# Hybrid decoder step: low parts subtracted before the next normalisation, the rest terms taken earlier, and the next layer's weight split behind the last normalisation

## Chip, cores and metric

The kernel runs on one core of a Trainium2 chip. The metric is the device time of one execution in microseconds (us).

## What is computed

The reference is one inference step of a 2-layer decoder for 512 prompt tokens and 64 sample tokens (8 sequences of 8), with D = 1024 channels. Cut to what matters here, each layer does

```python
mod = silu(c) @ w_ada[i] + b_ada[i]            # sh1, sc1, g1, sh2, sc2, g2
h = x * (1 + sc1) + sh1
mix = mixer(h @ w_in)                          # attention and convolution, then @ w_out
x = layernorm(ALPHA * x + g1 * mix)
h = x * (1 + sc2) + sh2
f = (silu(h @ w_gate) * (h @ w_up)) @ w_down
x = layernorm(ALPHA * x + g2 * f)
```

So there are four layer normalisations. The first three are each followed by a modulation of x to h and a projection of h, the last one by the output.

## The kernel before

**Layout.** Activations lie feature-major: `x` is 128 partitions x 8 tiles x 576 tokens. The two halves of 288 tokens are the columns of each matmul. All products are done in three parts to keep fp32 accuracy: weights and activations are split into a high part (a rounded copy, made by ScalarE) and a low part (the difference, made by VectorE), and TensorE adds high x high, low x high and high x low. A "unit" is one 128-column strip of weights over 8 tiles, 48 matmuls of 288 columns.

**Queues.** Each engine has its own order, written out by hand, and waits on semaphores. SyncE issues every transfer (`fetch` for weight units into the two buffers of `w_raw`, `around` for all else, among it the load of the layer's vectors `vec` after unit 1, which waits for `vec_used`). ScalarE makes `w_hi` (`split`, L500 to L507), which waits for the weights and for a free `w_hi` buffer of three. VectorE makes `w_lo` (`split`, L825 to L832), which frees the `w_raw` buffer for the next transfer.

**Normalisation.** The mean over the first six tiles is taken off early (`norm_first`). What is left of the mean, the rest, is subtracted by `take_rest` on VectorE, from sums in PSUM. `norm_last` on ScalarE loads the square root's table (L556), copies the row sums of squares (L558), squares the last tile (L547), squares the rest (L561) and takes the root (L563). VectorE takes the rest off tiles 0 to 2, reduces, takes the reciprocal (L966) and takes the rest off tiles 3 and 4. TensorE spreads the reciprocals over the partitions (L1310), and `normalise` multiplies each tile (L980). For tiles 5 to 7 it first takes the rest off that tile and waits for it.

**Modulation.** ScalarE scales the prompt tokens of a tile into one of three `hf` buffers (L519) and GpSimd the sample tokens (L463, L464); ScalarE rounds the tile to `h_hi` (L526); VectorE writes `h_lo` (L854), which frees the `hf` buffer. TensorE's `products_by_tile` (L1250) takes the tiles as their low parts come, for two units: 6 matmuls for each of tiles 0 to 3, 12 for each of tiles 4 to 7, and 24 for the second unit's last four tiles. `modulate` on VectorE puts the normalisations (`scale`) in between the low parts, two tiles ahead, and one weight split (`ahead`). For the first modulation of the kernel there is no normalisation and no split in it.

**Layer border.** After the last w_down product of layer 0, ScalarE makes the high part of layer 1's third unit (`split(l, UL + 2)`) and then `norm_last(l, 1)`. For the last layer that split returns at once.

Of the kernel before, what the change touches and what calls it, by code (L numbers as in the profile page):

```python
# [30 lines left out]
KT = D // P  # L31
# [77 lines left out]
NCEN = len(CENTRED)  # L109
# [41 lines left out]
def need(eng, sem, n):  # L151

    if n > 0:
        eng.wait_ge(sem, n)


def trunk(nc, xT, cT, ba_d, w_ada, w_mix, w_dn, kc_d, vc_d, st_d, vec_d, rope_d, eye_d, mp_d, msc_d, msn_d,
          y_d, k_d, v_d, cp_d, cs_d):
    with ExitStack() as ctx:
# [3 lines left out]
        s = {}  # L163
# [12 lines left out]
        def nth(l, name, k):  # L176

            return l * PER[name] + k + 1
# [106 lines left out]
        def halves(t):  # L285
            return t.rearrange("p (h n) -> p h n", h=2)
# [8 lines left out]
        def z_taken(l, z0, k):  # L295

            return l * ZL + z0 + k + 1
# [147 lines left out]
        def x_ready(eng, l, q, kt):  # L445

            if l == q == 0:
                eng.wait_ge(s["mod_ready"], 1)
                eng.wait_ge(x_in[kt // (KT // 2)], 16)
            else:  # L450
                eng.wait_ge(s["x_hat"], (2 * l + q - 1) * KT + kt + 1)
# [46 lines left out]
        def _(act):  # L498

            def split(l, u):  # L500

                g = l * UL + u
                if g >= DEPTH * UL:
                    return
                act.wait_ge(w_in[g % NR], 16 * (g // NR + 1))
                need(act, s["w_used"], g - NW + 1)
                nc.scalar.activation(w_hi[:, g % NW, :], w_raw[:, g % NR, :], ACT.Copy).then_inc(s["hi_ready"], 1)  # L507
# [5 lines left out]
            def modulate(l, q):  # L513

                def scaled(kt):

                    x_ready(act, l, q, kt)
                    need(act, s["h_lo"], (2 * l + q) * KT + kt + 1 - HF)
                    nc.scalar.activation(hf[:, kt % HF, 0:SEQ], x[:, kt, 0:SEQ], ACT.Identity, scale=h_mul[:, kt, 0:1],  # L519
                                         bias=h_add[:, kt, 0:1]).then_inc(s["h_f"], 1)  # L520

                def high(k):

                    act.wait_ge(s["h_f"], nth(l, "h_f", q * KT + k))
                    act.wait_ge(s["hs_f"], nth(l, "hs_f", q * KT + k))
                    nc.scalar.activation(h_hi[:, k, :], hf[:, k % HF, :], ACT.Copy).then_inc(s["h_hi"], 1)  # L526

                scaled(0)
                high(0)
                scaled(1)  # L530
                for kt in range(2, KT):
                    scaled(kt)
                    high(kt - 1)
                high(KT - 1)
# [6 lines left out]
            def squares(l, q, c):  # L541
                act.wait_ge(s["ln_cent"], nth(l, "ln_cent", NCEN * q + c))
                if c >= 3:
                    k = CENTRED[c][0]
                    act.wait_ge(z_free[k % 2], z_taken(l, (Z_OUT, Z_DN)[q], k // 2))
                part = slice(*CENTRED[c])
                nc.scalar.activation(SQ[q][:, part], x[:, part], ACT.Square).then_inc(s["ln_sq"], 1)  # L547

            def norm_first(l, q):

                act.wait_ge(s["ln_sum"], nth(l, "ln_sum", 2 * q))
                nc.scalar.activation(halves(MEAN[q][:]), MEAN_PS, ACT.Copy, scale=1.0 / (KM * P)).then_inc(s["ln_mean"], 1)

            def norm_last(l, q):

                nc.scalar.preload_act_table(ACT.Sqrt)  # L556
                act.wait_ge(s["ln_rows"], nth(l, "ln_rows", q))
                nc.scalar.activation(halves(rows[0:3 * GW, :]), ROWS_PS[0:3 * GW], ACT.Copy).then_inc(s["ln_rows_sb"], 1)  # L558
                squares(l, q, NCEN - 1)
                act.wait_ge(s["ln_sum"], nth(l, "ln_sum", 2 * q + 1))  # L560
                nc.scalar.activation(halves(rows[3 * GW:P, :]), REST_PS[3 * GW:P], ACT.Square, scale=1.0 / D).then_inc(s["ln_rest"], 1)  # L561
                act.wait_ge(s["ln_var"], nth(l, "ln_var", q))
                nc.scalar.activation(sd_col, var_col, ACT.Sqrt, bias=eps[0:TW]).then_inc(s["ln_sd"], 1)  # L563

            def ada_copy(k):

                act.wait_ge(s["ada_used"], 2 * k + 2)
                need(act, s["ada_t"], k)
                nc.scalar.activation(ada_o[:], ps[:, ada_banks(k // 2)[k % 2], :], ACT.Copy).then_inc(s["ada_sb"], 1)
# [83 lines left out]
            for l in range(DEPTH):  # L653

                for u in range(2):
                    if l == 0:
                        split(l, u)
                modulate(l, 0)
                if l == 0:
                    split(l, 2)  # L660
# [83 lines left out]
                for c in range(CT + 1):  # L744
# [6 lines left out]
                    if c:  # L751
                        k = c - 1
# [28 lines left out]
                split(l, OUT0 + KT + 2)  # L781
                norm_last(l, 0)
                modulate(l, 1)
                nc.scalar.preload_act_table(ACT.Silu)

# [14 lines left out]
                for m in range(KT):  # L800
                    for r in range(3):
                        u = DN0 + 3 * m + r
                        if r == 0 and l == 0 and m < 4:
                            ada_copy(DN_QUAD0 // 2 + m - 1)
                        if r == 2:
                            if m == KM:
                                norm_first(l, 1)
                            if m == KT - 2:
                                for c in range(NCEN - 1):
                                    squares(l, 1, c)  # L810
                        if u < UL - 1:
                            split(l, u + 3)
                split(l, UL + 2)
                norm_last(l, 1)
            for k in range(KT):
                act.wait_ge(s["x_hat"], (2 * DEPTH - 1) * KT + k + 1)
                restore(k, pend[:, 0], pend[:, 1])
# [2 lines left out]
        def _(dve):  # L820
# [23 lines left out]
            def modulate(l, q, ahead, scale=None):  # L844

                for kt in range(-2, KT + 1):
                    if scale and kt + 2 < KT:
                        scale(kt + 2)
                    if kt == 0 and len(ahead) > 1:
                        ahead[0]()  # L850
                    if kt > 0:
                        k = kt - 1
                        dve.wait_ge(s["h_hi"], nth(l, "h_hi", q * KT + k))
                        nc.vector.tensor_tensor(h_lo[:, k, :], hf[:, k % HF, :], h_hi[:, k, :].bitcast(F32), ALU.subtract)\  # L854
                            .then_inc(s["h_lo"], 1)
                    if kt == 1 and ahead:
                        ahead[-1]()

            def conv_tap(c):
# [90 lines left out]
            def take_rest(l, q, k):  # L950

                xk = halves(x[:, k, :])
                st.of(nc.vector.scalar_tensor_tensor(out=xk, in0=REST_PS, scalar=-1.0 / D, in1=xk, op0=ALU.mult, op1=ALU.add))  # L953

            def norm_last(l, q):

                for j in range(2):
                    dve.wait_ge(z_free[j], z_taken(l, (Z_OUT, Z_DN)[q], KT // 2 - 1))
                dve.wait_ge(s["ln_rest"], nth(l, "ln_rest", q))
                for k in range(3):  # L960
                    take_rest(l, q, k)
                dve.wait_ge(s["ln_cols"], nth(l, "ln_cols", q))
                nc.vector.tensor_reduce(var_col, COLS_PS.rearrange("p (c j) -> p j c", c=2), mybir.AxisListType.X, ALU.add)\
                    .then_inc(s["ln_var"], 1)
                dve.wait_ge(s["ln_sd"], nth(l, "ln_sd", q))
                nc.vector.reciprocal(rstd_col, sd_col).then_inc(s["ln_rcol"], 1)  # L966
                for k in range(3, 5):
                    take_rest(l, q, k)

            def normalise(l, q, k):  # L970
                if k == 0:
                    dve.wait_ge(s["ln_rstd"], nth(l, "ln_rstd", q))
                    st.wait(st.n)
                if k >= 5:
                    if k == KT - 1:
                        dve.wait_ge(s["ln_sq"], nth(l, "ln_sq", NCEN * q + NCEN - 1))
                    take_rest(l, q, k)
                    st.wait(st.n)
                xk = halves(x[:, k, :])
                nc.vector.tensor_tensor(xk, xk, RSTD_PS, ALU.mult).then_inc(s["x_hat"], 1)  # L980
# [82 lines left out]
            for l in range(DEPTH):  # L1063
                if l:
                    modulate(l, 0, [lambda: split(l, 2)], lambda k: normalise(l - 1, 1, k))
                    dve.wait_ge(s["x_hat"], nth(l - 1, "x_hat", 2 * KT - 1))
                    st.restart()
                else:
                    modulate(l, 0, [])
                    split(l, 2)  # L1070
# [63 lines left out]
                for c in range(CT):  # L1134
                    k = M_ORDER[c]
# [8 lines left out]
                for c in range(CT + 1):  # L1144
# [5 lines left out]
                    if c:  # L1150
                        k = M_ORDER[CT + c - 1]
# [625 lines left out]
```

## Time and profile before

| | |
|---|---|
| median of 3 runs | 1647.55 us (1645.03 to 1648.67) |
| profiled execution, its own time | 1650.15 us |
| its span | 1648.4 us |
| mean granted TensorE clock | 0.954 of full speed |

The span is what the trace covers; the execution's time lies 1.75 us above it. Rows of the trace carry the start in us from the span's start, the duration, the engine, the line and the operation.

### The profile page before, as it was taken

The numbers are of one execution on the slowest core, as the hardware profiler recorded it, in microseconds if no ns is written. First come the engines' busy times: TensorE is split into PE (matmuls) and PEld (weight loads), VectorE is DVE, ScalarE is ACT, GpSimd is POOL, SyncE is SP. The second block draws the span as 40 slices with busy tenths as digits, with TensorE's granted clock in tenths as the row PEclk, the third lists the DMA queues.
The fourth block names the chain that finished last, engine by engine and source line by source line (L and its number), as shares of the span: only waits on it lengthen the run. The fifth ranks groups of instructions, "written<-read, shape, count | busy, mean of one in ns | idle before, by whom it ended". The sixth has DMA issues, their size and how long they took to land.

```text
span 1648.4 us, 26440 instructions
## 1 busy us (share of the span) xinstructions
PE 1526.2 (93%) x11456; PEld 1380.1 (84%) x11456; DVE 790.7 (48%) x1246; ACT 561.6 (34%) x884; POOL 81.9 (5%) x104
## 2 busy tenths in 40 slices
PE   5999986889999999999978999868899999999996
PEld 3987754778999999999968977638799999999995
DVE  1789875554222222222327998865643333332233
ACT  3425565234322222211225255652342322221122
POOL 2000000101000000001001000001100000000100
PEclk7999998998999999999987999989889999999998
DMA  9575261422444444452213272512122222222221
GB/s 382 180 143 166 90 269 51 171 80 105 152 153 154 153 148 147 139 184 73 79 54 115 75 131 91 227 68 96 52 64 88 79 80 87 86 78 84 81 71 58
DMA packets 59523, 197.16 MB, mean 120 GB/s; under 512 B 22544, under 2 KB 22928, under 8 KB 48400
## 3 DMA queue, kind: packets, MB, share of 16 engines
q1 hardware_dynamic: 59408, 195.48, 35.7%
q8 instruction: 91, 1.49, 0.4%
q14 instruction: 24, 0.20, 0.0%
HBM read 187.27 MB, written 8.18 MB: 119 GB/s over the span
## 4 chain that ended last, share of the span: by engine, by line
PE 82%; DVE 11%; ACT 3%; issue 1%; DMA 1%; SPq 0%; DVEq 0%; ACTq 0%
PE ps L1230 66%; PE ps L1250 3%; PE ps L1321 3%; DVE sb_y L869 2%; DVE sb_x L980 1%; PE ps L1358 1%; PE ps L1332 1%; DMA sb_big<-w_ada 1%; ACT sb_E L588 1%; PE ps L1379 1%; PE ps L1587 1%; PE ps L1259 1%; DVE sb_x L953 1%; DVE sb_w_lo L831 1%; PE ps L1310 1%
## 5 line engine op out<-in xcount | busy, mean ns | idle before, releaser
L1230 PE MATMUL ps<-sb_h,sb_w_hi 128*128 128x288 f32 x4224 | 766.0, 297 | 3.0 <-DVE sb_x L920 3.0
L1230 PEld LDWEIGHTS ps<-sb_h,sb_w_hi 128*128 128x128 f32 x4224 | 623.1, 188 | 52.0 <-issue 47.4
L1230 PE MATMUL ps<-sb_h,sb_w_lo 128*128 128x288 f32 x2112 | 450.6, 294 | 0.0
L831 DVE TENSOR_TENSOR sb_w_lo<-sb_w_raw,sb_w_hi 128x1024 fp32r<-128x1024 f32 x192 | 235.7, 1229 | 375.5 <-ACT sb_w_hi L507 375.1
L1230 PEld LDWEIGHTS ps<-sb_h,sb_w_lo 128*128 128x128 f32 x2112 | 339.6, 188 | 0.0
L507 ACT ACTIVATE sb_w_hi<-sb_w_raw 128x1024 fp32r<-128x1024 f32 x192 | 202.1, 1053 | 324.1 <-PE ps L1230 290.5
L869 DVE SCALAR_TENSOR_TENSOR sb_y<-sb_uP,sb_vec,sb_y 128x512 f32<-128x512 f32 x240 | 164.8, 743 | 0.5
L1230 PE MATMUL ps<-sb_a_hi,sb_w_hi 128*128 128x288 f32 x704 | 151.9, 296 | 0.0
L1230 PE MATMUL ps<-sb_a_hi,sb_w_lo 128*128 128x288 f32 x704 | 150.1, 294 | 0.0
L1230 PE MATMUL ps<-sb_a_lo,sb_w_hi 128*128 128x288 f32 x704 | 149.6, 293 | 0.0
L795 ACT ACTIVATE sb_a_hi<-sb_af 128x576 fp32r<-128x576 f32 x44 | 30.2, 686 | 267.1 <-DVE sb_af L1185 267.1
L1185 DVE TENSOR_TENSOR sb_af<-ps,sb_gate 128x576 f32<-128x576 f32 x44 | 33.3, 758 | 181.1 <-PE ps L1230 178.8
L1230 PEld LDWEIGHTS ps<-sb_a_hi,sb_w_hi 128*128 128x128 f32 x704 | 112.3, 188 | 7.1 <-issue 6.9
L1230 PEld LDWEIGHTS ps<-sb_a_hi,sb_w_lo 128*128 128x128 f32 x704 | 112.9, 187 | 0.0
L1230 PEld LDWEIGHTS ps<-sb_a_lo,sb_w_hi 128*128 128x128 f32 x704 | 112.8, 187 | 0.0
L790 ACT ACTIVATE sb_gate<-ps 128x576 f32<-128x576 f32 x44 | 28.7, 652 | 162.0 <-PE ps L1230 153.6
L1250 PE MATMUL ps<-sb_h,sb_w_hi 128*128 128x288 f32 x256 | 59.8, 352 | 20.6 <-DVE sb_h L854 20.6
L1250 PEld LDWEIGHTS ps<-sb_h,sb_w_hi 128*128 128x128 f32 x256 | 47.7, 233 | 25.6 <-issue 14.5
L578 ACT ACTIVATE sb_E<-sb_E,sb_small 128x128 f32<-128x128 f32 (+3 forms) x64 | 35.5, 555 | 47.1 <-DVE sb_small L1018 46.4
L1587 PE MATMUL ps<-sb_h,sb_w_hi 128*128 128x288 f32 x128 | 28.0, 343 | 24.3 <-DVE sb_h L1137 16.0
L1187 DVE TENSOR_TENSOR sb_a_lo<-sb_af,sb_a_hi 128x576 fp32r<-128x576 f32 x44 | 33.4, 758 | 33.1 <-ACT sb_a_hi L795 33.1
L1379 PE MATMUL ps<-sb_eye,sb_E 128*128 128x128 f32 x160 | 30.8, 303 | 15.2 <-ACT sb_PT L597 7.0
(195 smaller groups left out, 1309.1 us busy)
## 6 DMA issues: line engine op xcount, KB each, us to landing
sb_w_raw<-w_mix SPq DMA_DIRECT2D x144, 512.0 KB, 3.5
sb_ring<-w_ada SPq DMA_DIRECT2D x40, 1024.0 KB, 5.8
sb_w_raw<-w_dn SPq DMA_DIRECT2D x32, 512.0 KB, 3.5
sb_ring<-vc_d SPq DMA_DIRECT2D x12, 1024.0 KB, 6.9
sb_big<-w_ada SPq DMA_DIRECT2D x8, 1024.0 KB, 12.2
sb_ring<-kc_d SPq DMA_DIRECT2D x8, 1024.0 KB, 7.4
sb_w_raw<-w_dn SPq DMA_DIRECT2D x16, 384.0 KB, 3.2
sb_cache_a<-kc_d SPq DMA_DIRECT2D x4, 1024.0 KB, 8.0
```

What stands on the lines that cost most here:

```text
L507: nc.scalar.activation(w_hi[:, g % NW, :], w_raw[:, g % NR, :], ACT.Copy).then_inc(s["hi_ready"], 1)
L578: nc.scalar.activation(blk, blk, ACT.Exp, bias=nm8[p % 2][:, c:c + 1], scale=SCALE, accum_out=den8[p % 2][:, c:c + 1]).then_inc(s["exp_rea ...
L795: nc.scalar.activation(a_hi[:, i], af[:], ACT.Copy).then_inc(s["a_hi"], 1)
L831: nc.vector.tensor_tensor(w_lo[:, g % NW, :], w_raw[:, g % NR, :], w_hi[:, g % NW, :].bitcast(F32), ALU.subtract)\
L869: ins = nc.vector.scalar_tensor_tensor(out=yp, in0=up, scalar=tap, in1=yp, op0=ALU.mult, op1=ALU.add)
L1185: nc.vector.tensor_tensor(halves(af[:]), Z[1], halves(gate[:]), ALU.mult).then_inc(z_free[1], 1)
L1187: nc.vector.tensor_tensor(a_lo[:, i], af[:], a_hi[:, i].bitcast(F32), ALU.subtract).then_inc(s["a_lo"], 1)
L1230: ins = nc.tensor.matmul(z[:, i], a[:, g % NW, w], b[:, k0 + k, i * H:(i + 1) * H], start=first and k == 0 and t == 0, stop=last and k == ...
L1250: ins = nc.tensor.matmul(Z[u][:, i], a[:, j, w], b[:, k, i * H:(i + 1) * H], start=n == 0 and t == 0, stop=n == KT - 1 and t == 2)
L1321: ins = nc.tensor.matmul(ps[j * GW:(j + 1) * GW, ada_banks(sec)[g], :], c_in[:, NG * half + j, :], buf[:, j * 512:(j + 1) * 512], start=ha ...
L1379: ins = nc.tensor.transpose(ps[:, 6 + j % 2, (q - k) * P:(q - k + 1) * P], E[:, e, o:o + P], eye[:])
L1587: ins = nc.tensor.matmul(Z[u][:, i], a[:, j, w], b[:, k, i * H:(i + 1) * H], start=n == 0 and t == 0, stop=n == KT - 1 and t == 2)
```

## The change

Four edits. ScalarE's `modulate` makes the high part of tile 1 before it scales tile 2. At the end of a layer ScalarE does `norm_last(l, 1)` first and the split of the next layer's third unit after it. VectorE's `modulate` subtracts the low part of a tile before the next normalisation and not after it, and makes the weight split at step 4 (behind the low part of tile 3 and the normalisation of tile 6) in place of step 1. VectorE takes the rest off tiles 3 to 6 behind the reciprocal, in place of tiles 3 and 4, so that only tile 7 does it inside `normalise`.

```diff
-                scaled(0)
-                high(0)
-                scaled(1)
-                for kt in range(2, KT):
+                for kt in range(2):
+                    scaled(kt)
+                    high(kt)
+                scaled(2)
+                for kt in range(3, KT):
                     scaled(kt)
                     high(kt - 1)
                 high(KT - 1)
...
+                norm_last(l, 1)
                 split(l, UL + 2)
-                norm_last(l, 1)
...
                 for kt in range(-2, KT + 1):
-                    if scale and kt + 2 < KT:
-                        scale(kt + 2)
-                    if kt == 0 and len(ahead) > 1:
-                        ahead[0]()
                     if kt > 0:
                         k = kt - 1
                         dve.wait_ge(s["h_hi"], nth(l, "h_hi", q * KT + k))
                         nc.vector.tensor_tensor(h_lo[:, k, :], hf[:, k % HF, :], h_hi[:, k, :].bitcast(F32), ALU.subtract)\
                             .then_inc(s["h_lo"], 1)
-                    if kt == 1 and ahead:
+                    if scale and kt + 2 < KT:
+                        scale(kt + 2)
+                    if kt == 4 and ahead:
                         ahead[-1]()
...
-                for k in range(3, 5):
+                for k in range(3, KT - 1):
                     take_rest(l, q, k)
...
-                if k >= 5:
-                    if k == KT - 1:
-                        dve.wait_ge(s["ln_sq"], nth(l, "ln_sq", NCEN * q + NCEN - 1))
+                if k == KT - 1:
+                    dve.wait_ge(s["ln_sq"], nth(l, "ln_sq", NCEN * q + NCEN - 1))
                     take_rest(l, q, k)
                     st.wait(st.n)
```

## Rows read from the trace of the kernel before

**Rows 1.** The page, part 1: busy time, share of the span, instructions.
```profile
PE 1526.2 (93%) x11456; PEld 1380.1 (84%) x11456; DVE 790.7 (48%) x1246; ACT 561.6 (34%) x884; POOL 81.9 (5%) x104
```

**Rows 2.** The chain that ended last, around the layer border: start, length, what.
```profile
832.28 12.89 PE ps L1230 x96
...
847.24 1.80 PE ps L1230 x12
...
851.50 4.37 DMA sb_w_raw<-w_mix
...
856.96 1.28 ACT L556
```

**Rows 3.** Timeline of the layer border: start, length, engine, line, idle before.
```profile
849.99 0.22 DVE L934 TENSOR_TENSOR sb_x<-sb_x,sb_gate 128x64 f32<-128x64 f32 x1
...
855.89 1.06 ACT L507 ACTIVATE sb_w_hi<-sb_w_raw 128x1024 fp32r<-128x1024 f32 x1 [12.73 <-DMA sb_w_raw<-w_mix]
...
867.31 2.75 DVE L980 TENSOR_TENSOR sb_x<-sb_x,ps 128x576 f32<-128x576 f32 x4 [1.67 <-PE ps L1310]
```

**Rows 4.** Waits of SyncE's queue, 820 to 900 us: total, times, longest.
```profile
SPq L381 <- DVEq L1211: 20.5, 1, 20.5
```

**Rows 5.** Timeline of the last normalisation and the output.
```profile
1628.48 0.22 DVE L934 TENSOR_TENSOR sb_x<-sb_x,sb_gate 128x64 f32<-128x64 f32 x1
...
1633.07 0.30 ACT L563 ACTIVATE sb_cols<-sb_cols,sb_small 96x6 f32<-96x6 f32 x1 [2.33 <-DVE sb_cols L963]
...
1633.51 1.38 DVE L953 SCALAR_TENSOR_TENSOR sb_x<-ps,sb_x 128x576 f32<-128x576 f32 x2
...
1636.45 3.41 DVE L980 TENSOR_TENSOR sb_x<-sb_x,ps 128x576 f32<-128x576 f32 x5 [1.57 <-PE ps L1310]
1637.24 3.90 ACT L538 ACTIVATE sb_x<-sb_x,sb_pend 128x576 f32<-128x576 f32 x5 [3.88 <-DVE sb_x L980]
1638.89 6.60 SPq L439 DMA_DIRECT2D y_d<-sb_x  x4
...
1644.27 0.87 ACT L538 ACTIVATE sb_x<-sb_x,sb_pend 128x576 f32<-128x576 f32 x1 [0.59 <-DVE sb_x L980]
```

**Rows 6.** Timeline of the modulation behind the layer border.
```profile
868.10 0.81 ACT L519 ACTIVATE sb_hf<-sb_x,sb_h_add,sb_h_mul 128x512 f32<-128x512 f32 x1 [3.98 <-DVE sb_x L980]
...
868.95 0.68 ACT L526 ACTIVATE sb_h<-sb_hf 128x576 fp32r<-128x576 f32 x1
...
869.98 0.78 DVE L854 TENSOR_TENSOR sb_h<-sb_hf,sb_h 128x576 fp32r<-128x576 f32 x1
870.69 1.22 DVE L831 TENSOR_TENSOR sb_w_lo<-sb_w_raw,sb_w_hi 128x1024 fp32r<-128x1024 f32 x1
...
870.91 1.15 POOL L463 TENSOR_TENSOR sb_hf<-sb_x,sb_h_mul 128x64 f32<-128x64 f32 x1 [0.76 <-DVE sb_h L854]
...
880.37 0.69 PE L1250 MATMUL ps<-sb_h,sb_w_lo 128*128 128x288 f32 x2
880.85 1.17 PE L1250 MATMUL ps<-sb_h,sb_w_hi 128*128 128x288 f32 x4
```

**Rows 7.** The chain that ended last, tile 4 on, two of three stretches.
```profile
879.75 11.14 PE ps L1250 x72
...
1203.47 11.39 PE ps L1250 x72
```

**Rows 8.** Window behind the border: us, busy per engine, clock, DMA share, GB/s.
```profile
870.90:890.70 19.80, 18.15 (x96) 16.80 (x97) 11.93 (x16) 11.00 (x16) 5.29 (x12) 0.70 0.23 46
```

**Rows 9.** Timeline of the first modulation of the kernel.
```profile
34.51 0.69 POOL L464 TENSOR_TENSOR sb_hf<-sb_hf,sb_h_add 128x64 f32<-128x64 f32 x1
...
35.29 0.68 ACT L526 ACTIVATE sb_h<-sb_hf 128x576 fp32r<-128x576 f32 x1
...
40.34 0.91 PE L1250 MATMUL ps<-sb_h,sb_w_hi 128*128 128x288 f32 x4
40.72 0.30 PEld L1250 LDWEIGHTS ps<-sb_h,sb_w_hi 128*128 128x128 f32 x2 [0.18 <-issue]
```

## Prediction

> **What bounds the kernel now.** I read the page first. TensorE has matmuls in flight for 93% of the span [rows 1], so only stretches in which it waits or runs at its low clock can give time back. The chain of waits then shows where those are: at full speed it repeats pieces of 96 matmuls in 12.89 us, 0.134 us each [rows 2], and the breaks that the diff touches are the four places where h is made for a new projection, and the end.
>
> The worst is the border between layers. The chain goes from TensorE's last w_down product, which ends at 849.04, over a weight transfer at 851.50 that takes 4.37 us, to a table load at 856.96 [rows 2]. The timeline says why. The row sums that ScalarE is to copy are made ahead of the product's last 12 matmuls, so they were ready at 847.24 [rows 2], and the last residual tile at 850.21, but ScalarE sat behind the high part of layer 1's third unit until 855.89, because that unit's weights had not landed [rows 3]. They were late because SyncE, in order, stood 20.5 us before the load of `vec`, which waits for VectorE's last reading of the old one [rows 4]. The first normalisation starts only at 867.31 [rows 3].
>
> The end of the kernel is the same normalisation with no split in the way [rows 5]. From the end of the last residual addition (1628.70) to the first normalisation (1636.45) it takes 7.75 us. At the border this distance is 867.31 - 850.21 = 17.10 us.
>
> Behind each normalisation comes a stretch in which the eight tiles pass VectorE (normalise), ScalarE (scale, high part), VectorE (low part) and TensorE (96 matmuls, 6 for each of tiles 0 to 3, 12 for tiles 4 to 7, 24 to finish). At the border TensorE starts tile 4 at 879.75, 12.44 us after the first normalisation, and needs 11.14 us for the 72 matmuls that are left; of the other two stretches the longer needs 11.39 [rows 7]. At 0.134 us they would be 9.67: the granted clock averages 0.70 in the stretch [rows 8], and pairs start 0.48 us apart (0.24 per matmul, the 1.2 GHz level) [rows 6].
>
> **Change, part 1: norm_last before the split (layer border only; for the last layer that split does nothing).** The sqrt table load, the row copy and the last squares no longer stand behind the transfer. Table load and copy go under the last product, as at the end of the kernel. VectorE's residual still ends at 850.21, so with the distance of rows 5 the first normalisation starts at 850.21 + 7.75 = 857.96 in place of 867.31: 9.35 us less. The split is not gone. Its transfer is issued as before (it waits for VectorE, not ScalarE) and lands by 855.87. ScalarE's square root ends 4.67 us after the residual at the end of the kernel [rows 5], so here at 854.9; the split runs 855.89 to 856.95 [rows 3], and the next work of ScalarE, scaling tile 0, needs the normalised tile at 857.96 + 0.75 = 858.71. Cover: 1.76 us. Every further us of lateness of the transfer beyond that comes back as a wait ahead of all eight tiles. A table load takes 1.28 us in rows 2, and the copy begins at once after it. The Trainium skill, "ScalarE: Activation LUTs", section "What ACT_TABLE_LOAD costs", adds a drain of about 1.38 us to each load; by that page taking the load off the path would be worth 2.66 us of the 9.35, by the row 1.28, and the sum is the same since it is taken from the distance and not from the parts.
>
> **Part 2: rest terms (take_rest) of tiles 5 and 6 taken ahead.** Two VectorE operations of 0.69 us (two in 1.38) [rows 5] go behind the reciprocal, where VectorE stands 1.57 to 1.67 us waiting for TensorE to spread the reciprocals [rows 3, 5]. Four then take about 2.75 us from 1633.51, to 1636.26, against 1636.45: covered by 0.2 us. Without that cover it costs 1.4 us at each of four places. In return the stretches lose two of three pairs of rest term, drain and normalise (tile 7 keeps its own, since its square must be read first).
>
> **Part 3: low part before the next normalisation, split(2) moved from tile 0 to tile 3.** I worked out the stretch as a recursion in the issue order of each engine, time 0 at the first normalisation. Durations [rows 3, 6]: scaling 0.81, high part 0.68, low part, normalise and rest term 0.75, split 1.22; an operation that waits starts 0.045 behind what it waits for, one that does not starts 0.085 before its predecessor ends; scaling tile k needs the low part of tile k-3; TensorE starts 0.15 behind a low part. With the old order the low parts start at 2.66, 5.12, 7.25, 9.37 and 11.50; the trace has 2.67 for the first [rows 6] and tile 4 on TensorE at 12.44 against 12.40 by recursion, so it holds to 0.1 us. With the new order: normalise 0 to 2 end at 2.09; low 0 waits only for its high part and starts at 2.38; high 1 ends at 3.78, low 1 starts at 3.83; then 5.87, 7.20, the split, 9.66, rest term and normalisation of tile 7, 11.79, 13.37, 14.03. Tile 4 reaches TensorE at 9.66 + 0.90 = 10.56 in place of 12.44.
>
> From there TensorE has 72 matmuls. If they take as long as before the gain is 1.9 us. If the clock is up from tile 4 on, the arrivals of tiles 5 and 6 set the pace and the end falls at 20.7 in place of 879.75 + 11.14 - 867.31 = 23.6: 3.0 us with the longer two counted in. If tiles 4 and 5 run wholly at the low clock the end is 10.56 + 24 x 0.24 + 48 x 0.134 = 22.75: 0.9 us. (Before, 11.39 - 9.67 = 1.7 us is 16 slow matmuls at 0.106 us more each.) TensorE's holes ahead of tile 4 shrink from 3 x 0.7 us (2.13 a tile against 1.44 of work at the low clock) to about 1.5 us in all, so I put the rise a little earlier than before and take 2.3 us, three times: 6.9 us, with 2.7 and 9.0 as ends.
>
> The split of the third unit ends at about 9.7 in place of 4.6. Behind it in SyncE's queue stand the transfer of the unit two further on and, in layer 0, an adaLN quarter. With 4.37 us of transfer the weights are there at 14.1, and TensorE frees the w_hi buffer they need only when both first units are done, past 20: nothing. GpSimd's sample part is stretched when VectorE runs beside it (1.15 us beside the split, 0.69 beside a low part [rows 6, 9]). The new order puts split and low part together, and tile 5's sample part may end near 11.4 instead of 9; its high part is needed by 11.75. Nothing, but with 0.3 us to spare; without it some 0.7 us a stretch, which TensorE's backlog hides mostly.
>
> **Part 4: ScalarE's order in the very first stretch (no normalisation there).** High 1 now stands before scaling 2. There GpSimd finishes tile 1's sample part only at 35.20, and high 1 started at 35.29 with the two scalings done before it [rows 9]. Now ScalarE idles until 35.24 and scaling 2 comes behind: all later tiles move by one overlapped scaling, 0.7 us. TensorE reached tile 4 at 40.72 after 0.18 us of waiting [rows 9] and had no backlog, so I count the whole 0.7 as loss.
>
> **Part 5: the tail.** Normalisations start 0.67 us apart up to tile 6, then the rest term and tile 7 start at 4.7 and 5.5. ScalarE's restoring (0.78 us apart) ends at about 0.79 + 7 x 0.78 + 0.87 = 7.1 in place of 1645.14 - 1636.45 = 8.7 [rows 5]. The output transfers then follow at 1.56 us, which four of 576 KB can keep, so 1.5 us arrive at the end.
>
> **Sum.** 9.35 + 6.9 - 0.7 + 1.5 = 17.05 us. The profiled execution took 1650.15 (span 1648.4), so 1633.1; the median of the runs shown is 2.6 lower, at 1647.55, hence 1630.5.
>
> **Rivals.** (a) *Clock up early:* 3 x 3.0 in place of 6.9, 1628.4. For it: the first stretch of the kernel, nearly without holes, was at full speed by 40.34 (four matmuls in 0.91 us with a wait of 0.18 in it, against 1.17 without one at the low clock) [rows 6, 9]. (b) *Clock up late:* full-speed work on one tile takes 0.8 us and tiles come every 1.3 to 2.5 us, so TensorE may be granted the low clock until well into the continuous work: 3 x 0.9, 1634.7. The Trainium skill, "TensorE: Matmul & The Clock Gate", section "HAM oscillation — how this bites in real kernels", says that bursts with waits between them pay the low clock again and again; by that rule this case holds. (c) *The wait returns* ahead of scaling 0, since the transfer still cannot start before 851.5: if it lands x us later than 1.76 us after 855.87 the border gives 9.35 - x; with all of it gone 1639.8. Against it: start and size of the transfer are untouched, and it landed 2.8 us before it is needed. (d) *Slower:* the low clock holds through the three stretches and into the products behind. Each matmul at 0.24 costs 0.106 us more, so it needs (17.05 + 3.3) / 0.106, about 190 more slow matmuls, two whole stretches, to come out over 0.2% slower; twice that, 380, gives 1670. Against it: the products behind have no hole. (e) *No effect:* the chain that I read is not the one that binds, 1647.5; rows 2 and 3 agree too well for it.
>
> **Chances.** Forecast 0.62 (own range 1628.7 to 1633), (a) 0.12, (b) 0.18, (c) 0.05, (d) 0.02, (e) 0.01. A change under 0.2% (3.3 us) is about what a measurement of this kernel cannot tell from none. So faster 0.97, within 0.2% 0.01, slower 0.02. Range: (a) and (b) with the runs' spread of 2 us either side, 1626.5 to 1635.5.
>
> **What would show it.** In the new profile: the copy L558 of the border before 849 and the first normalisation there near 858; the split near 855.9 ahead of the first scaling, with no ScalarE wait after it; four rest terms in one run and TensorE's spread still the releaser of the first normalisation; low parts at 2.4, 3.8, 5.9, 7.2 behind it and 72 matmuls from 10.6; the first stretch's tile 4 at 41.4; the last restoring 7.1 us after the last first normalisation. The prediction fails if the transfer at the border lands after 857.6, if the rest terms hold the first normalisation, or if the granted clock of the stretches falls under 0.7.

## The result, and the profile after

The changed kernel takes 1631.13 us (median of 4 runs, 1629.58 to 1631.47), the kernel before 1647.26 (4 runs, 1645.03 to 1648.67). The ratio is 0.9901 with a 95% interval of 0.9884 to 0.9919: 16.1 us less, where 17.05 were forecast. The profiled execution of the changed kernel took 1630.94 us, with a span of 1629.1. The line numbers of the changed kernel differ by one or two.

The page's line of busy times, to set beside [rows 1]. TensorE has 9 us less in flight for the same matmuls; the mean granted clock is 0.963 in place of 0.954:

```profile
PE 1517.5 (93%) x11456; PEld 1373.7 (84%) x11456; DVE 790.6 (49%) x1246; ACT 561.4 (34%) x884; POOL 85.8 (5%) x104
```

The timeline of the layer border in the changed kernel, for [rows 3]. Start, length, engine, line, operation, and in brackets the idle time before and its releaser:

```profile
839.10 1.28 ACT L557 ACT_TABLE_LOAD   x1
...
843.22 0.65 ACT L559 ACTIVATE sb_rows<-ps 96x576 f32<-96x576 f32 x1 [2.84 <-PE ps L1289]
...
845.91 0.22 DVE L933 TENSOR_TENSOR sb_x<-sb_x,sb_gate 128x64 f32<-128x64 f32 x1
...
847.42 16.73 SPq L349 DMA_DIRECT2D sb_w_raw<-w_mix  x3
...
850.94 2.70 DVE L952 SCALAR_TENSOR_TENSOR sb_x<-ps,sb_x 128x576 f32<-128x576 f32 x4
...
851.24 1.06 ACT L507 ACTIVATE sb_w_hi<-sb_w_raw 128x1024 fp32r<-128x1024 f32 x1 [0.45 <-DMA sb_w_raw<-w_mix]
854.09 2.08 DVE L978 TENSOR_TENSOR sb_x<-sb_x,ps 128x576 f32<-128x576 f32 x3 [0.46 <-PE ps L1308]
854.88 0.81 ACT L519 ACTIVATE sb_hf<-sb_x,sb_h_add,sb_h_mul 128x512 f32<-128x512 f32 x1 [2.58 <-DVE sb_x L978]
```

Table load and copy now lie under the last product. The first normalisation follows the residual (846.13) after 7.96 us in place of 17.10. The weights still come late (asked for at 847.42, the first of the three issues in that row; split at 851.24), but nobody stands behind the split: before the first scaling ScalarE waits 2.58 us for VectorE. A part of the gain is the clock's. Before, TensorE had stood idle for 8.05 us until 859.62, its next small matmuls ran at the low clock, and VectorE's reduction waited 1.26 us for them:

```profile
859.62 2.05 PE L1302 MATMUL ps<-sb_small,sb_sq_h 128*96 128x1 f32 x12 [8.05 <-ACT sb_sq_h L547]
861.53 2.06 PE L1305 MATMUL ps<-sb_small,sb_rows 128*96 128x1 f32 x12
863.62 0.17 DVE L963 TENSOR_REDUCE sb_cols<-ps 96x6 f32<-96x12 f32 x1 [1.26 <-PE ps L1305]
```

In the changed kernel the same two groups take 1.10 and 1.16 us, and the reduction waits for nothing of TensorE. So about 1.3 of the 9.1 us at the border is the low clock behind TensorE's long wait. The clock can be low there in a short border too: in split last (below) the second group takes 2.06 us, but VectorE's rest terms still run beside it, and the first normalisation comes 8.12 us behind the residual, against 7.96.

SyncE's wait itself is as long as in [rows 4]:

```profile
SPq L381 <- DVEq L1209: 20.5, 1, 20.5
```

The four rest terms end at 853.64, and TensorE is still the releaser, with 0.46 us to spare.

The chain that ended last, from the point where TensorE no longer waits in each stretch, for [rows 7]:

```profile
379.56 8.20 PE ps L1248 x60
...
864.71 11.30 PE ps L1248 x72
...
1188.92 8.21 PE ps L1248 x60
```

And the windows of the three stretches, for [rows 8] (window, length, busy time and instructions of each engine, mean granted clock as a share of full, DMA share, GB/s):

```profile
370.20:387.80 17.60, 15.34 (x100) 14.20 (x104) 11.37 (x16) 11.28 (x16) 5.70 (x10) 0.91 0.28 93
857.30:876.00 18.70, 16.89 (x98) 16.14 (x99) 11.44 (x15) 11.36 (x16) 6.85 (x13) 0.80 0.26 51
1179.50:1197.10 17.60, 16.28 (x98) 15.52 (x99) 11.42 (x15) 11.34 (x16) 5.74 (x11) 0.83 0.10 32
```

In the first and third the 60 matmuls behind tile 4 run at the full rate (0.137 us each), so the chain begins at tile 5: arrival sets the end. In the second, tile 4 ran at 0.25 us a matmul, and the 72 take 11.30 us, about as before. The same view in smaller windows shows that the clock there had come up and fell again just as tile 4 began:

```profile
857.30:861.30 4.00, 3.81 (x14) 3.49 (x15) 3.44 (x6) 3.79 (x6) 1.78 (x5) 0.50 0.00 0
861.30:864.70 3.40, 1.78 (x12) 1.34 (x11) 3.40 (x6) 2.72 (x4) 2.93 (x4) 1.00 0.00 0
864.70:868.10 3.40, 3.40 (x14) 3.40 (x15) 2.58 (x4) 2.03 (x4) 1.05 (x3) 0.50 0.46 154
868.10:876.00 7.90, 7.90 (x62) 7.90 (x61) 2.02 (x3) 2.81 (x3) 1.09 (x2) 1.00 0.42 55
```

In the first stretch TensorE stood just as long ahead of tile 4, and the granted clock stayed at 1.00 from 373.2 on. What made the difference is not shown.

The timeline of the stretch behind the border, for [rows 6]:

```profile
856.45 0.76 DVE L851 TENSOR_TENSOR sb_h<-sb_hf,sb_h 128x576 fp32r<-128x576 f32 x1 [0.27 <-ACT sb_h L526]
...
862.58 1.21 DVE L832 TENSOR_TENSOR sb_w_lo<-sb_w_raw,sb_w_hi 128x1024 fp32r<-128x1024 f32 x1
...
863.71 0.85 DVE L851 TENSOR_TENSOR sb_h<-sb_hf,sb_h 128x576 fp32r<-128x576 f32 x1
...
864.71 0.81 PE L1248 MATMUL ps<-sb_h,sb_w_hi 128*128 128x288 f32 x2 [1.61 <-DVE sb_h L851]
```

The split stands directly ahead of the low part of tile 4, and TensorE waits 1.61 us for that low part. Not all of it is the split's: with the split last (below) the wait at the same place is 0.69 us.

The tail, for [rows 5]:

```profile
1618.82 4.74 DVE L978 TENSOR_TENSOR sb_x<-sb_x,ps 128x576 f32<-128x576 f32 x7 [0.34 <-PE ps L1308]
1619.61 6.31 ACT L539 ACTIVATE sb_x<-sb_x,sb_pend 128x576 f32<-128x576 f32 x8 [3.98 <-DVE sb_x L978]
1621.26 5.02 SPq L439 DMA_DIRECT2D y_d<-sb_x  x4
```

Restoring runs without a hole and ends at 1625.92, 7.10 us behind the first normalisation in place of 8.69.

Where the 19.2 us between the two spans (1648.35 and 1629.14) went, by the same marks in both traces:

| part | before | after | less |
|---|---|---|---|
| start to end of the first stretch | 50.51 | 49.00 | 1.5 |
| stretch in layer 0 (first normalisation to last matmul) | 23.74 | 20.84 | 2.9 |
| last product's end (849.04, 844.96) to first normalisation, border | 18.27 | 9.13 | 9.1 |
| stretch behind the border | 23.58 | 21.92 | 1.7 |
| stretch in layer 1 | 23.83 | 20.86 | 3.0 |
| last first normalisation to the end | 11.90 | 10.32 | 1.6 |
| all between these | 1496.5 | 1497.1 | -0.6 |

The 1.5 us of the start are not the change's. In the profiled execution of before, TensorE's last products for the modulation ran at the low clock (granted 0.50 between 24 and 31.6 us), and scaling began at 31.61; in the changed kernel, and in every experiment, with ScalarE's old order and with its new one, it began between 29.80 and 30.79, released by the transfer of `x`. That execution, 1650.15 us, was also above all four runs of the median.

### The profile page after: what moved, and what is told of

Its sections match the earlier page's. It is cut to its first block, busy times and chain, and to the rows that moved or that the text cites. A ratio compares the mean times of both kernels' runs of the same rounds, so it can differ in the third digit from the quotient of the medians.

```text
span 1629.1 us, 26440 instructions
## 1 busy us (share of the span) xinstructions
PE 1517.5 (93%) x11456; PEld 1373.7 (84%) x11456; DVE 790.6 (49%) x1246; ACT 561.4 (34%) x884; POOL 85.8 (5%) x104
## 4 chain that ended last, share of the span: by engine, by line
PE 82%; DVE 10%; ACT 4%; issue 2%; DMA 1%; SPq 0%; POOL 0%; DVEq 0%; ACTq 0%; POOLq 0%
PE ps L1228 67%; PE ps L1248 2%; PE ps L1319 2%; DVE sb_y L868 2%; DMA sb_x<-xT 1%; PE ps L1356 1%; ACT sb_E L589 1%; PE ps L1585 1%; PE ps L1377 1%; PE ps L1257 1%; PE ps L1330 1%; DVE sb_x L978 1%; DVE sb_w_lo L832 1%; PE ps L1308 1%; DVE sb_h L851 1%
## 5 line engine op out<-in xcount | busy, mean ns | idle before, releaser
L1248 PE MATMUL ps<-sb_h,sb_w_hi 128*128 128x288 f32 x256 | 55.4, 334 | 20.2 <-DVE sb_h L851 19.8
```

What stands on the lines that cost most here:

```text
L1248: ins = nc.tensor.matmul(Z[u][:, i], a[:, j, w], b[:, k, i * H:(i + 1) * H], start=n == 0 and t == 0, stop=n == KT - 1 and t == 2)
```

## The experiments

Each was timed in 5 rounds beside the kernel before; the changed kernel's row is that of the result. "Stretches" are the three times from the first normalisation to the last matmul of `products_by_tile`; "low parts" are starts behind the first normalisation.

| kernel | ratio to before | 95% | median us | stretches us |
|---|---|---|---|---|
| changed kernel | 0.9901 | 0.9884 to 0.9919 | 1631.13 | 20.84, 21.92, 20.86 |
| border only | 0.9947 | 0.9933 to 0.9960 | 1637.35 | 22.20, 23.93, 22.95 |
| vec later | 0.9954 | 0.9941 to 0.9966 | 1638.89 | 22.20, 23.21, 23.76 |
| all but border | 0.9946 | 0.9933 to 0.9958 | 1638.04 | 20.85, 20.86, 20.86 |
| rest only | 0.9941 | 0.9929 to 0.9954 | 1637.88 | 20.81, 21.24, 20.82 |
| low first only | 0.9974 | 0.9963 to 0.9984 | 1643.26 | 21.63, 22.75, 21.64 |
| ScalarE order only | 0.9998 | 0.9989 to 1.0007 | 1646.97 | 22.20, 23.06, 23.74 |
| split at 1 | 0.9890 | 0.9876 to 0.9904 | 1629.98 | 20.39, 20.37, 20.37 |
| split last | 0.9880 | 0.9866 to 0.9893 | 1626.99 | 19.93, 19.95, 19.94 |
| normalisation first, split last | 0.9874 | 0.9861 to 0.9887 | 1627.32 | 19.97, 19.98, 19.97 |
| reordered | 0.9869 | 0.9855 to 0.9883 | 1625.43 | 18.83, 18.92, 18.84 |

**Border only.** The kernel before with

```diff
-                split(l, UL + 2)
                 norm_last(l, 1)
+                split(l, UL + 2)
```

> The kernel before with only the border edit: norm_last(l, 1) ahead of the next layer's split. Theory (the split stood behind a late transfer, and with it the whole normalisation): first normalisation at the border 8.0 us behind the last residual in place of 17.1, so 9.1 us less, ratio 0.9945; the other three stretches as before. Rival (the wait returns ahead of scaling tile 0, or the low clock eats it): under 3 us, ratio above 0.998.

Distance from residual to first normalisation: 7.86 us, ratio 0.9947. The theory holds, and its number too (0.9945).

**Vec later.** ScalarE as before, and on SyncE in layer 1 the load of `vec` behind the fetch of the third unit:

```diff
-                if u == 1:
+                if u == (2 if l else 1):
                     need(sp, s["vec_used"], l)
```

> The kernel before, unchanged on ScalarE, with one edit on SyncE: in layer 1 the load of vec stands behind the fetch of the third unit in place of ahead of it, so that unit's weights are asked for about 14 us earlier. Theory (of the 9.1 us at the border nearly all is the late transfer, and ScalarE's order matters only because of it): the split runs from 849.1 to 850.2, then table load, copy and squares as in the other normalisations with a split ahead, where residual to first normalisation is 8.12 us, so the first normalisation comes 8.9 us earlier, ratio 0.9946. Rival (the split's own 1.06 us and the table load of 1.28 behind it are a large part): at most 6 us, ratio 0.9965 or more.

The ratio is 0.9954, the distance 9.45 us in place of 17.10: 7.65 of the 9.14 us come back without touching ScalarE. So the order was harmful because of what the split waited for. The timeline of that kernel shows the rest:

```profile
846.95 1.06 ACT L507 ACTIVATE sb_w_hi<-sb_w_raw 128x1024 fp32r<-128x1024 f32 x1 [5.97 <-PE ps L1230]
...
848.02 1.28 ACT L556 ACT_TABLE_LOAD   x1
...
851.69 2.06 PE L1305 MATMUL ps<-sb_small,sb_rows 128*96 128x1 f32 x12
...
857.48 2.75 DVE L980 TENSOR_TENSOR sb_x<-sb_x,ps 128x576 f32<-128x576 f32 x4 [1.67 <-PE ps L1310]
```

Split and table load keep the last squares until 849.86, 1.83 us behind the residual (0.10 in border only: 847.64, 847.74). TensorE's 12 small matmuls take 2.06 us, at a granted clock of 0.50 between 851.7 and 853.8; in border only the same 12 take 1.16 us at 1.00. VectorE stands 0.36 us for them. So 8.12 us was forecast and 9.45 measured. I had taken the distance from the first normalisation of layer 0, where the last squares start 0.98 us behind the residual and these matmuls take 1.16 us.

**All but border.** The changed kernel with the two lines of ScalarE put back.

> The changed kernel with the split put back ahead of norm_last(l, 1). Theory (the edits add up): 9.1 us slower than the changed kernel, that is about 7.5 to 9 us below the kernel before (three stretches 2 to 3 us each, tail 1.6), ratio 0.9948; at the border the first normalisation comes 17.3 us behind the residual. Rival (the edits need each other, since rest terms and low parts only matter when the border is short): less than 5 us below before, ratio above 0.997.

0.9946. With border only it makes 0.9893 of the two against 0.9901 together: the two groups of edits add up within their intervals. The border keeps 16.59 us from residual to first normalisation.

**Rest only.** The kernel before with

```diff
-                for k in range(3, 5):
+                for k in range(3, KT - 1):
                     take_rest(l, q, k)
...
-                if k >= 5:
-                    if k == KT - 1:
+                if k == KT - 1:
```

> The kernel before with only the rest edit: the rests of tiles 3 to 6 taken behind the reciprocal. Theory (two rest terms leave each stretch and hide in the wait for TensorE): first normalisation at the same distance from the residual, low parts at 2.66, 5.12, 6.46, 7.79, 9.91 behind it (before: 2.67, 5.18, 7.30, 9.42, 11.55), ends of the stretches between 20.5 and 22.3 by the clock, against 22.2 to 23.9 with the old code; tail 1.6 us shorter; in all 6.4 us, ratio 0.9961. Rival (the four rest terms reach past the reciprocals' arrival): first normalisation 1.4 us later at four places, ratio 0.999 to 1.000.

0.9941: the theory's direction, but 9.7 us (7.6 to 11.7) in place of 6.4. By the traces it is 6.7 us in the three stretches, against the mean of those with the old order (23.2, below), and 1.6 us in the tail. The low parts came within 0.25 us of what was expected (2.67, 5.18, 6.51, 7.94, 10.16), the first normalisation did not move. In its timeline the holes between tiles shrink, and tile 4 reaches TensorE at 377.83, 11.06 us behind the first normalisation at 366.77:

```profile
373.28 0.84 DVE L854 TENSOR_TENSOR sb_h<-sb_hf,sb_h 128x576 fp32r<-128x576 f32 x1
...
374.71 0.85 DVE L854 TENSOR_TENSOR sb_h<-sb_hf,sb_h 128x576 fp32r<-128x576 f32 x1
...
377.83 0.50 PE L1249 MATMUL ps<-sb_h,sb_w_hi 128*128 128x288 f32 x2 [0.80 <-DVE sb_h L854]
```

Two matmuls in 0.50 us, against 0.81 at the same place behind the border in the changed kernel: the clock was up. From there TensorE has no hole left, so the arrival of tile 4 sets the end.

**Low first only.** The kernel before with VectorE's low part ahead of the normalisation, split left behind tile 0:

```diff
                 for kt in range(-2, KT + 1):
-                    if scale and kt + 2 < KT:
-                        scale(kt + 2)
                     if kt > 0:
                         ...
+                    if scale and kt + 2 < KT:
+                        scale(kt + 2)
                     if kt == 1 and ahead:
```

> The kernel before with only VectorE's order in modulate changed: the low part of a tile ahead of the next normalisation, the split left behind tile 0. Theory: low parts at 2.38, 4.84, 6.17, 8.29, 10.42, tile 4 on TensorE about 1.1 us earlier, stretches 0.6 to 1.1 us shorter each, 2.5 us in all, ratio 0.9985; it is the smaller part of the gain in the stretches. Rival (this edit, the first named in the change, carries the stretches): 5 us or more, ratio 0.997 or less.

0.9974 lies between theory and rival: 4.3 us. The low parts came at 2.35, 4.83, 6.26, 8.38, 10.51, within 0.1 us of what was expected, and the stretches are 1.2 us shorter than the mean of those with the old order (23.2, below). By itself the edit is worth about half of the rest edit.

**Split at 1** and **split last.** The changed kernel with `kt == 1`, and with `kt == KT`, in place of `kt == 4`.

> The changed kernel with the weight split back behind tile 0 (step 1). Theory (the split delays whatever stands behind it, and at step 4 that is the tile with 12 matmuls): low parts at 2.38, 4.84, 6.17, 7.75, 9.08, 11.20, stretches end at 20.2 in place of 20.8, so 1.7 us less than the changed kernel in all, ratio to before 0.9891. Rival (moving the split away from the first tiles is part of the gain): slower than the changed kernel, 0.9915 or more.

> The changed kernel with VectorE's weight split at the end of modulate (behind the last low part) in place of behind tile 3. Theory (the 1.22 us of the split stand ahead of the low part of tile 4, and TensorE waits there): low part of tile 4 starts 8.8 us behind the first normalisation in place of 9.6, the stretches end at 19.9 in place of 20.7 with the clock up, so 0.7 to 0.9 us less in each of three, 2.5 us in all, ratio to before 0.9887. Rival 1 (the low clock or the arrivals of tiles 5 to 7 set the end): no change against the changed kernel, 0.9901. Rival 2 (the later split delays SyncE's next transfer and a product waits for weights): slower than the changed kernel by 1 us or more per stretch, 0.992.

Step 1: 20.4 us in all three stretches where 20.2 was expected, and 0.9890; against the changed kernel's 0.9901 the intervals overlap, so it is the traces that decide. Step 8: 19.9, as expected, and 0.9880. No later transfer was missed: from the end of the first stretch to the first normalisation at the border it takes 466.5 us, against 466.3 in the changed kernel. The chosen step 4 is the worst of the three: it stands ahead of the first tile with 12 matmuls, and the low part of tile 5 comes at 11.84, against 11.38 at step 1 and 10.92 at step 8. In split last TensorE waits 0.01 to 0.69 us ahead of tile 4, where it waits 0.95 to 1.61 us in the changed kernel. The rows show the 0.21 us between tile 4 and tile 5, whose low part is the first row, and the split as the last:

```profile
377.13 0.75 DVE L851 TENSOR_TENSOR sb_h<-sb_hf,sb_h 128x576 fp32r<-128x576 f32 x1
...
377.94 0.53 PE L1248 MATMUL ps<-sb_h,sb_w_hi 128*128 128x288 f32 x2 [0.21 <-DVE sb_h L851]
...
380.01 1.22 DVE L832 TENSOR_TENSOR sb_w_lo<-sb_w_raw,sb_w_hi 128x1024 fp32r<-128x1024 f32 x1
```

**Normalisation first, split last.** As split last, but the low-part edit taken back:

```diff
+                    if scale and kt + 2 < KT:
+                        scale(kt + 2)
                     if kt > 0:
                         ...
-                    if scale and kt + 2 < KT:
-                        scale(kt + 2)
-                    if kt == 4 and ahead:
+                    if kt == KT and ahead:
```

> The changed kernel without its low-part edit (normalisation before the low part again, as in the kernel before) and with the split last. Theory (the low-part edit gives nothing once the rest terms are gone and the split stands last, since the order in which VectorE does two short operations moves tile 4 by less than the split did): low parts at 2.66, 3.99, 5.87, 7.20, 9.32, 9.99, stretches end at 19.9, the same as with low parts first and the split last (19.9), ratio 0.988. Rival (low parts ahead of normalisations are worth their own 1 us a stretch): stretches end at 20.9, ratio 0.990.

19.97 against 19.94 us, and 0.9874 against 0.9880: no difference. The edit trades one arrival for another. With low parts first tile 4 reaches TensorE at 9.7 and tile 5, whose low part starts at 10.92, sets the end. With normalisations first tile 4 comes at 10.22, the low part of tile 5 starts at 9.99, and TensorE has no hole from tile 4 on. So the low-part edit gives nothing beside the rest edit when the split stands last. With the split at step 1 it does give something, though no run takes it alone: rest only (20.8 us with the clock up) and split at 1 (20.4) differ in it and in ScalarE's order.

**ScalarE order only.**

```diff
-                scaled(0)
-                high(0)
-                scaled(1)
-                for kt in range(2, KT):
+                for kt in range(2):
+                    scaled(kt)
+                    high(kt)
+                scaled(2)
+                for kt in range(3, KT):
```

> The kernel before with only ScalarE's order in modulate changed (high part of tile 1 ahead of scaling tile 2). Theory (VectorE normalises four tiles before the first low part, so nothing changes in the three stretches; in the first stretch of the kernel the low parts behind tile 1 move by 0.1 to 0.4 us, not by the 0.7 predicted, unless GpSimd is late as it was in the profiled execution of before): low parts at 2.67, 5.17, 7.30 as before, ratio 1.000. Rival (0.7 us or more lost in the first stretch and some in each other): ratio 1.001 or more, and low part of tile 2 in the first stretch more than 2 us behind that of tile 1.

0.9998 (0.9989 to 1.0007), an interval that is too wide to exclude 0.7 us, so the traces decide. The low parts of the three stretches are those of before. In the first stretch the one of tile 1 comes 0.6 us earlier and the one of tile 2 0.14 later behind tile 0's, and from the first low part to the last matmul it takes 16.66 us, against 16.71 in border only and 16.77 in vec later with the old order: nothing is lost. This edit was tested with VectorE's old order only; what it does beside the low-part edit no run takes apart.

**Reordered.** An order for which the recursion of the prediction gives an end at 18.7: split last; the rest term of tile 7 between the low parts of tiles 4 and 5; its normalisation behind that of tile 5; each high part right behind its scaling.

```diff
-                for kt in range(2):
+                n = 2 if l == q == 0 else KT - 1
+                for kt in range(n):
                     scaled(kt)
                     high(kt)
...
-                    if scale and kt + 2 < KT:
+                    if scale and kt + 2 < KT - 1:
                         scale(kt + 2)
-                    if kt == 4 and ahead:
+                    if scale and kt + 2 in (KT - 1, KT):
+                        scale(KT - 1, kt + 2 == KT - 1, kt + 2 == KT)
+                    if kt == KT and ahead:
...
```

> The changed kernel with the split last, the rest of tile 7 between the low parts of tiles 4 and 5 and its normalisation behind that of tile 5, and ScalarE making each tile's high part right behind its scaling (in the three stretches with a normalisation). Theory (the arrival of tiles 4 and 5 at TensorE sets the end of a stretch once the clock is up; the recursion gives low parts of tiles 4 and 5 0.5 to 1.2 us earlier): the stretches end at 18.7 to 18.9, against 19.9 with the split last alone, 3 to 3.6 us less in all, ratio 0.9860. Rival (GpSimd's sample part, which each high part now waits for sooner, or the low clock takes the place): no gain over the split last alone, 0.9880.

The stretches end at 18.83 to 18.92, low parts every 1.42 us up to tile 6. The ratio, 0.9869, is the lowest of all, but its interval overlaps that of split last, so the last step is shown by the traces (1.1 us a stretch; from the first normalisation of layer 0 to the end of the span 1255.5 against 1258.2 us) and not by the medians. GpSimd is near: its first operation on a tile takes 0.72 to 0.84 us in place of 0.30 beside each low part, and its results are still in time.

```profile
371.94 0.83 POOL L463 TENSOR_TENSOR sb_hf<-sb_x,sb_h_mul 128x64 f32<-128x64 f32 x1 [0.59 <-DVE sb_x L984]
...
377.02 0.51 PE L1254 MATMUL ps<-sb_h,sb_w_hi 128*128 128x288 f32 x2 [0.43 <-DVE sb_h L852]
```

## Why the prediction was right

**Part 1, border (9.35 us): right, 9.1.** The mechanism is shown from two sides, by moving the waiting work out of the queue (border only) and by moving the transfer (vec later). The first normalisation fell 7.96 us behind the residual where 7.75 was taken. Rival (c), the wait coming back, did not occur: the split ended 2.58 us before the first scaling. ScalarE's copy began 0.01 us behind the table load in vec later (848.02 + 1.28, 849.31), so the drain of 1.38 us that the Trainium skill, "ScalarE: Activation LUTs", section "What ACT_TABLE_LOAD costs", adds to each load is not seen here. In the changed kernel the load lies under TensorE's product.

**Part 2, rest terms: covered, as predicted**, with 0.34 to 0.46 us to spare where 0.2 was worked out. But I gave this part no number of its own, and it carries the stretches: alone it brings them to 20.8 to 21.2 us, and with them gone the low-part edit is worth little (normalisation first, split last).

**Part 3, the recursion: right to 0.1 us.** Low parts forecast at 2.38, 3.83, 5.87, 7.20, 9.66, 11.79, 13.37; measured 2.36, 3.78, 5.76, 7.15, 9.62, 11.84, 13.38. The three stretches: 6.9 us forecast, 7.5 between the two profiled executions. That is somewhat lucky. Stretches with the old order end, in 12 cases of four traces (before, border only, vec later, ScalarE order only), between 22.20 and 23.93 us, 23.2 in the mean; the three of before were 23.7. With the new order six cases (changed kernel, all but border) are 20.84 to 20.86 and once 21.92, 21.0 in the mean. Three times 2.2 is 6.5 us, nearer to the medians: 9.1 + 6.5 + 1.6 = 17.2, and 16.1 (13.3 to 19.1) measured.

What I did not see is which edit earns it. Rest terms alone 21.0 in the mean, low first alone 22.0, both together with the split at step 4 21.0. With the split left at step 1 both (and ScalarE's order) give 20.4, so moving it to step 4 cost about 0.5 us a stretch. Even so the two do not add (2.2 and 1.2 us alone, 2.8 together). Behind the last low part the split gives another 0.4 us: 19.9, with either order of low part and normalisation.

**Rivals (a) and (b), the clock.** Both show: the first and third stretch of the changed kernel are case (a) (20.7 forecast, 20.85 measured), the second (21.92) is over half way to case (b), 22.75. In that one the granted clock was at 1.00 from 861.3, went back to 0.50 at 864.7, after a wait of 1.61 us, and was at 1.00 again from 868.1. All but border has the same order and the same wait in its second stretch; there the clock stayed up, and it took 20.86 us. Over whole stretches, with holes of 0.1 to 1.6 us, the granted clock was 0.80 to 0.91 in the stretches, above the 0.70 behind the border before.

The Trainium skill, "TensorE: Matmul & The Clock Gate", section "HAM oscillation — how this bites in real kernels", tells of bursts of matmuls with waits of 3 to 5 us for a transfer between them, which pay the low clock each time. The waits inside these stretches are shorter, so that by the page alone I should not have said that case (b) holds; the trace shows the low clock paid again in one of three.

Rival (d) is excluded by the same rows: from 868.1 on the clock is at 1.00. The upper end of my range was also short of what it is said to hold: (b) gives 1634.7, and with 2 us of spread 1636.7, not 1635.5. The measured 1631.13 lies inside both.

**Part 4, the first stretch: wrong, 0.7 us of loss that are not there.** The step that failed is that GpSimd finishes tile 1's sample part only at 35.20. That was a collision of one execution: there VectorE's two weight splits began together with scaling (31.67 and 31.61), and GpSimd's work on tiles 0 and 1 stood beside them. In the other traces scaling waits for `x` until about 30, the splits are at most beside tile 0, and GpSimd is done with tile 1 before ScalarE needs it, as in the changed kernel:

```profile
30.01 0.32 POOL L463 TENSOR_TENSOR sb_hf<-sb_x,sb_h_mul 128x64 f32<-128x64 f32 x1 [29.56 <-DMA sb_x<-xT]
...
31.89 0.30 POOL L464 TENSOR_TENSOR sb_hf<-sb_hf,sb_h_add 128x64 f32<-128x64 f32 x1
...
33.07 0.68 ACT L526 ACTIVATE sb_h<-sb_hf 128x576 fp32r<-128x576 f32 x1
```

Tile 1's sample part is ready at 32.19, its high part starts at 33.07, right behind its scaling. ScalarE order only shows the same, 16.66 us from the first low part to the last matmul against 16.71 with the old order.

**Part 5, the tail: right.** 7.10 us to the end of restoring, as worked out; 1.6 us at the end where 1.5 was forecast.

The sum came out 0.9 us from the median. A loss of 0.7 that is not there and slightly too much at border (9.35 for 9.1) and stretches (6.9 for 6.5) cancel, and that is luck.

## What to carry to other kernels

When an engine stands long in a wait, look at what is queued behind the waiting instruction, and then at who delays the thing it waits for: here either cure, reordering ScalarE or SyncE, gave most of the 9 us. For a pipeline of tiles over several engines, write down each engine's order with measured durations and follow it by hand: it gave the starts of the changed kernel to 0.1 us and those of the experiments to 0.25. The experiments then showed that one 1.22 us operation costs most directly ahead of the first tile with 12 matmuls (0.9 us a stretch against its best place, behind the last tile). Undo the edits of a bundle one at a time, since here low parts first gave nothing once the rest terms were gone and the split stood last, and the moved split, hidden among the others, cost 0.5 us a stretch.

## What the runs showed of the hardware

The same instruction order took between 22.20 and 23.93 us for one stretch, in executions of nearly the same kernel, by the moment at which the granted clock rose to stay: 9.8 us behind the first normalisation it took 22.20 us (border only, vec later and ScalarE order only, first stretch), 14.1 us behind it 22.95 and 16.3 us behind it 23.93 (border only, third and second). With the split last it varied less (19.93 to 19.98 in six cases), and there the clock was up before tile 4 in all six. Of TensorE's 12 small matmuls (128x1) in the normalisation, 1.16 us at the high clock became 2.06 at the low one. An operation of GpSimd on 64 columns takes 0.30 us, also beside VectorE's normalisations, which read PSUM. Where it is stretched beside a low part of VectorE it takes 0.68 to 0.89, and beside a weight split up to 1.28 (1.14 to 1.21 in the three stretches); VectorE's own low part beside it went from 0.75 to at most 0.87.
